# Latent and differential attention of a layer in one software pipeline of one stage, in place of two stages

## What is computed

```
def blocked_attention(q, k, v, scale):          # mla_group: 8 heads, 96 wide, values 64 wide
    def block(qb):
        s = jnp.einsum('bqhd,bkhd->bhqk', qb, k).astype(jnp.float32) * scale
        p = jax.nn.softmax(s, axis=-1).astype(v.dtype)
        return jnp.einsum('bhqk,bkhd->bqhd', p, v)
    return from_query_blocks(lax.map(block, to_query_blocks(q)))

def diff_group(dq, dk, dv, lam, lam_init, g_sub, cos, sin):   # 4 heads, 2 softmaxes each, 32 wide
    ...
    def block(qb):
        sc = jnp.einsum('bqhcd,bkhcd->bhcqk', qb, k).astype(jnp.float32) * scale
        p = jax.nn.softmax(sc, axis=-1)
        a = (p[:, :, 0] - lam * p[:, :, 1]).astype(v.dtype)
        return jnp.einsum('bhqk,bkhe->bqhe', a, v)
```

## Time and profile before

| | |
|---|---|
| median of 3 runs | 3117.5 us (3116.7 to 3121.64) |
| the profiled execution | 3118.45 us, of which its span in the profile is 3116.6 us |
| TensorE busy | 2902.9 us, 93% of the span |
| VectorE busy | 1549.0 us, 50% |
| ScalarE busy | 1204.4 us, 39% |
| GpSimd busy | 332.8 us, 11% |
| mean granted TensorE clock | 0.969 |

### The profile page before, as it was taken

The page is one execution under the profiler, slowest core; times in us unless marked ns, Lnnn a source line. Parts: engine busy times, 40 slices in busy tenths (PEclk is TensorE's granted clock), DMA queues, the critical chain, the costliest instruction groups (busy, mean ns, idle before and its releaser), DMA issues. The chain is left out here.

```text
span 3116.6 us, 38710 instructions
## 1 busy us (share of the span) xinstructions
PE 2902.9 (93%) x14576; PEld 2288.1 (73%) x14576; DVE 1549.0 (50%) x2177; ACT 1204.4 (39%) x1797; POOL 332.8 (11%) x286
## 2 busy tenths in 40 slices
PE   6999887999989999899899989999899899899998
PEld 2888765688868888586587768887675577678886
DVE  3467256565544443456753455443465663444434
ACT  3642434632233332434543343333424552333333
POOL 0010004500001100003000121100104001011100
PEclk8999999999999999999899999999999899999999
DMA  6100210045412222120032122222120131122232
GB/s 238 68 28 1 88 54 1 11 166 166 158 68 96 104 97 95 64 81 15 28 111 93 54 70 105 95 104 82 69 82 1 41 135 55 54 95 94 94 105 94
DMA packets 43552, 254.04 MB, mean 82 GB/s; under 512 B 4608, under 2 KB 6784, under 8 KB 15872
## 3 DMA queue, kind: packets, MB, share of 16 engines
q1 hardware_dynamic: 43392, 251.87, 22.7%
HBM read 249.75 MB, written 2.10 MB: 81 GB/s over the span
## 5 line engine op out<-in xcount | busy, mean ns | idle before, releaser
L250 DVE TENSOR_TENSOR ring_lo<-ring,ring_hi 128x2048 fp32r<-128x2048 f32 x201 | 460.7, 2292 | 796.3 <-ACT ring_hi L243 796.0
L243 ACT ACTIVATE ring_hi<-ring 128x2048 fp32r<-128x2048 f32 x201 | 383.8, 1909 | 462.1 <-PE bank L301 341.8
L301 PE MATMUL bank<-h_hi,ring_hi 128*128 128x512 f32 x1360 | 541.1, 398 | 19.4 <-DVE ring_lo L250 8.5
L301 PE MATMUL bank<-h_hi,ring_lo 128*128 128x512 f32 x1360 | 532.5, 392 | 0.0
L1435 PE MATMUL bank<-h_hi,ring_hi 128*128 128x512 f32 x960 | 374.1, 390 | 5.7 <-DVE ring_lo L250 5.7
L1439 PE MATMUL bank<-h_hi,ring_lo 128*128 128x512 f32 x960 | 373.5, 389 | 0.0
L1438 PE MATMUL bank<-h_lo,ring_hi 128*128 128x512 f32 x960 | 373.5, 389 | 0.0
L301 PEld LDWEIGHTS bank<-h_hi,ring_hi 128*128 128x128 f32 x1360 | 257.2, 189 | 79.4 <-issue 16.7
L301 PEld LDWEIGHTS bank<-h_hi,ring_lo 128*128 128x128 f32 x1360 | 257.1, 189 | 54.4
L301 PE MATMUL bank<-h_lo,ring_hi 128*128 128x512 f32 x624 | 243.9, 391 | 0.0
L1435 PEld LDWEIGHTS bank<-h_hi,ring_hi 128*128 128x128 f32 x960 | 180.2, 188 | 45.3 <-issue 5.5
(11 more groups left out here) (442 smaller groups left out, 4929.8 us busy)
## 6 DMA issues: line engine op xcount, KB each, us to landing
ring<-in_stream SPq DMA_DIRECT2D x209, 1024.0 KB, 4.8
mod_w<-in_stream SPq DMA_DIRECT2D x64, 256.0 KB, 4.6
xT<-in_xT SPq DMA_DIRECT2D x2, 2048.0 KB, 14.6
const<-in_const SPq DMA_DIRECT2D x1, 2306.5 KB, 15.7
par<-in_par SPq DMA_DIRECT2D x3, 696.0 KB, 4.0
memT<-in_memT SPq DMA_DIRECT2D x2, 1024.0 KB, 4.9
out<-xT SPq DMA_DIRECT2D x1, 2048.0 KB, 6.2
ctxT<-in_ctxT SPq DMA_DIRECT2D x1, 1024.0 KB, 4.9
```

The costliest lines, as they stand in the source:

```text
L243: nc.scalar.activation(self.slab_hi(slab + j), self.slab(slab + j), ACT.Copy).then_inc(slab_rounded, 1)
L250: nc.vector.tensor_tensor(lower, self.slab(slab + j), self.slab_hi(slab + j).bitcast(F32), ALU.subtract)\
L301: ins = nc.tensor.matmul(out, lhsT, rhs, start=start and w is w_hi and x is x_hi, stop=stop and w is w_lo)
```

## The change

`differential_attention` goes, and `two_attentions` takes its place, called once a layer instead of the two stages. In iteration i of one loop it issues a step of latent unit i or its predecessors and a step of differential unit i or its predecessors, on each engine. What each unit computes, and on which engine, stays. New buffers: the latent units have `probs` in the first half of `raw` and the differential ones in the second half (`raw` is free at this point; `squares2` isn't used any more), and a statistics tile each. PSUM is divided: banks 0 and 1 hold the scores of one latent unit, 2 and 3 those of one differential unit, bank 4 takes in turn the transposed tiles of latent head 0 and of the differential unit, bank 5 those of latent head 1, 6 and 7 the sums. So each kind has room for the scores of one unit instead of two. The score matmuls and maxima of the latent units signal head by head.

The diff, cut to its core (bodies of steps that only got new names are left out, and so are the removed lines, which stand in the listing above):

```diff
-        def differential_attention(name, dq, dk, dv, read_out, work, neg_lam):
+        def two_attentions(name, latent, dq, dk, dv, read_latent, read_diff, work, neg_lam):
             N = 4 * TB
-            S_ = lambda u: bank[:, 2 * (u % 2):2 * (u % 2) + 2, :]
+            probs, probsT, stat, diff_probs, diff_probsT, diff_stat = work
+            OUT, DIFF_OUT = 6, 7
...
             def tensor(pe):
                 def scores(u):
+                    for g in range(2):
+                        if u > 0:
+                            pe.wait_ge(exp_done.sem, exp_done.at(2 * (u - 1) + g + 1))
+                        lhsT, rhs = latent[u]["scores"][g]
+                        nc.tensor.matmul(bank[:, g, :], lhsT, rhs, start=True, stop=True).then_inc(scored.sem, 1)
+
+                def diff_scores(u):
                     n, tb, g = place_of(u)
-                    if u >= 2:
-                        pe.wait_ge(exp_done.sem, exp_done.at(u - 1))
+                    if u > 0:
+                        pe.wait_ge(diff_exp_done.sem, diff_exp_done.at(u))
...
                 def transposes(u):
+                    for g in range(2):
+                        pe.wait_ge(probs_ready.sem, probs_ready.at(2 * u + g + 1))
+                        if u > 0:
+                            if g == 0:
+                                pe.wait_ge(diff_out.sem, diff_out.at(u))
+                            else:
+                                pe.wait_ge(probs_out[1].sem, probs_out[1].at(u))
...
+                def diff_transposes(u):
+                    pe.wait_ge(probs_out[0].sem, probs_out[0].at(u + 1))
+                    pe.wait_ge(diff_ready.sem, diff_ready.at(u + 1))
...
+                def values(u):
+                    t, tb = divmod(u, TB)
+                    for g in range(2):
+                        pe.wait_ge(probs_out[g].sem, probs_out[g].at(u + 1))
...
+                for i in range(N + 2):
+                    if i < N:
+                        scores(i)
+                    if i >= 2:
+                        diff_transposes(i - 2)
+                        values(i - 2)
+                    if i < N:
+                        diff_scores(i)
+                    if 1 <= i <= N:
+                        transposes(i - 1)
+                    if i >= 3 and i % 2:
+                        diff_values(i - 3)
...
             def scalar(act):
...
+                for i in range(N + 1):
+                    if i < N:
+                        exps(i)
+                    if i >= 1:
+                        copy(i - 1)
+                    if i < N:
+                        diff_exps(i)
+                    if i >= 1:
+                        diff_copy(i - 1)
...
             def vector(dve):
...
+                for i in range(N + 2):
+                    if i >= 2:
+                        copy(i - 2)
+                        if (i - 2) % TB == 0 and i > 2:
+                            turn_out((i - 2) // TB - 1)
+                    if i < N:
+                        maxima(i)
+                    if 1 <= i <= N:
+                        differences(i - 1)
+                    if i < N:
+                        diff_maxima(i)
+                        inverses(i)
+                    if i == 2 * TB + 2:
+                        diff_turn_out(0)
+                turn_out(3)
+                diff_turn_out(1)
+
+            def gpsimd(pool):
                 for u in range(N):
+                    pool.wait_ge(inverse_ready.sem, inverse_ready.at(u + 1))
...
-                    paired_attention("latent", 4, unit_of, lambda t: mix[:, t, :],
-                                     (probs, spare[:, 0:4, :].rearrange("p (u h) n -> p u (h n)", u=2), stat), 2, (4, 5), (6, 7),
-                                     ("act", "dve"))
-                    differential_attention("differential", dq, dk, dv, lambda n: mix[:, 6 + n, :],
-                                           (probs, spare[:, 4:8, :], stat), neg_lam)
+                    two = lambda x, first: x[:, first:first + 4, :].rearrange("p (u h) n -> p u h n", u=2)
...
+                    two_attentions("attention", units, dq, dk, dv, lambda t: mix[:, t, :], lambda n: mix[:, 6 + n, :],
+                                   (two(raw, 0), two(h_spare, 0), stat, two(raw, 4), h_spare[:, 4:8, :], diff_stat), neg_lam)
```

More of the change, by code:

```diff
@@ L1279, in transposes @@
-                    if u >= 2:
-                        pe.wait_ge(probs_out.sem, probs_out.at(u - 1))
+                    for g in range(2):
[5 more added lines that the diff above has]
+                                pe.wait_ge(probs_out[1].sem, probs_out[1].at(u))
+                        for j in range(TB):
+                            last = nc.tensor.transpose(bank[:, 4 + g, j * P:(j + 1) * P], probs[:, u % 2, g, j * P:(j + 1) * P], con("ident"))
+                        last.then_inc(turned[g].sem, 1)
@@ L1286, in values @@
                 def values(u):
+                    t, tb = divmod(u, TB)
+                    for g in range(2):
+                        pe.wait_ge(probs_out[g].sem, probs_out[g].at(u + 1))
+                    if tb == 0 and t > 0:
+                        pe.wait_ge(sum_read.sem, sum_read.at(t))
+                    for j, sides in enumerate(latent[u]["values"]):
+                        for g in range(2):
+                            last = nc.tensor.matmul(bank[g * HD:(g + 1) * HD, OUT, tb * P:(tb + 1) * P], sides[g],
+                                                    probsT[:, u % 2, g, j * P:(j + 1) * P], start=j == 0, stop=j == TB - 1)
@@ L1293, in values @@
                                                     start=j == 0, stop=j == TB - 1)
                     if tb == TB - 1:
[L1295 to L1305, removed]
+                        last.then_inc(diff_summed.sem, 1)
@@ L1320, in scalar, with diff_copy @@
[L1320 to L1325, removed]
+                    act.wait_ge(turned[0].sem, turned[0].at(u + 1))
+                    nc.scalar.activation(probsT[:, u % 2, 0, :], bank[:, 4, :], ACT.Copy).then_inc(probs_out[0].sem, 1)
+                def diff_copy(u):
+                    act.wait_ge(diff_turned.sem, diff_turned.at(u + 1))
+                    nc.scalar.activation(diff_probsT[:, u % 4, :], bank[:, 4, :], ACT.Copy).then_inc(diff_out.sem, 1)
@@ L1343, in vector @@
                 nc.vector.memset(stat[:, :, :, :], 0.0)
+                nc.vector.memset(diff_stat[:, :, :, :], 0.0)
                 dve.drain()
[L1345 to L1353 removed]
```

120 lines of the change are left out of this document (77 added, 43 removed).

## The result

The changed kernel takes **3074.1 us** (median of 4 runs, 3072.5 to 3077.4), the kernel before 3118.8 beside it (3116.7 to 3121.6): a ratio of 0.9859, 95% interval 0.9848 to 0.9871. Measured again beside other kernels it took 3074.1, ratio 0.9859 (0.9844 to 0.9874).

A forecast was written before the change was run, and what follows sets the result against it. TensorE was taken to bound the first stage, VectorE the second, and TensorE the merged one: 16 x 6.01 + 2.3 = 98.5 us, saving 17.5 and 17.8, 35.3 together, giving 3082 us. The range was 3075 to 3097.

The forecast's parts named there:

- the waits (a) to (e): New stage: five TensorE waits, for differential and latent scores, latent transposes and two shared-bank copies, each taken as 0.
- An iteration is 3.81 + 2.20 = 6.01 us: New stage, TensorE: 3.81 us for a latent unit plus 2.20 for a differential unit make one iteration.
- The ways in and out, 2.3 us: New stage's edges: 0.9 us idle at the start, about 0.5 of waits and 0.9 through read-out at the end.
- VectorE has 1.16 us of room: New stage: VectorE needs 4.85 us an iteration against TensorE's 6.01, leaving 1.16.
- GpSimd and VectorE don't cost each other anything: New stage: VectorE's difference beside GpSimd's multiplying was taken to cost 0; upper end 2 x 1.03 us an iteration.
- the rival's price, 6.91 against 6.01: Every iteration: VectorE becomes the bound through GpSimd, 14.4 us a layer, 3111 us in all; chance 0.05.
- The clock stays up in the stage: New stage: TensorE at full clock, cost 0; upper end 6.8 us a layer.
- Behind the stage nothing is gained: Head of the next stage: no gain despite half clock, since TensorE waits there for VectorE's tiles.
- a next stage of another length as a sign of being wrong: Behind the new stage: a next stage taking another time than now would show the prediction wrong.
- the clock did not fall at the start: Rival, stage start: clock falls for 13.65 us a layer, costing 6.8 us each, 3096 us; chance 0.12.
- the pipelines do interleave: Rival said they don't: a ring of waits holds every iteration at about 7.1 us, 3118 us; chance 0.04.
- the 37% at half clock: Rival, new stage: clock as low as in the differential stage, 121 us a layer, 3128 us; chance 0.04.

The follow-up runs named there:

- e5: The changed kernel with one unused 128x512 matmul more on TensorE in 14 iterations of each layer: 3097.2 us, ratio 0.9928.
- e3: The changed kernel with the differential values moved directly behind the latent values on TensorE: 3069.1 us, ratio 0.9844; again 3070.3, 0.9846.
- e7: The changed kernel with three unused 128x512 reductions more on VectorE behind each unit's inverses: 3099.3 us, ratio 0.9935.
- e4: The changed kernel with VectorE's difference moved behind the unit's maxima and the inverse that releases GpSimd: 3151.1 us, ratio 1.0100.
- e10: The changed kernel with VectorE's difference moved behind the differential maxima but ahead of the inverses: 3083.8 us, ratio 0.9890.
- e1: The kernel before with unused TensorE matmuls in the differential stage, three at its start, one in each iteration, one at its end: 3107.6 us, ratio 0.9968.
- e2: The kernel before with only three unused TensorE matmuls, where the differential stage waits for its first exponentials: 3114.7 us, ratio 0.9986.
- e9: The changed kernel with differential values directly behind latent values and five unused 128x512 matmuls behind the stage's last values: 3076.2 us, ratio 0.9866.

## Why the prediction was right in kind and short in size

- *TensorE is the bound, and the waits (a) to (e) are hidden.* Right: no wait in 14 iterations, and e5's added work is paid in full.
- *An iteration is 3.81 + 2.20 = 6.01 us.* **The mis-sized term**: 5.87, which over 2 x 16 is 4.5 of the missing 9.3 us. The parts came from rows in which each group had another neighbour than it has now. The groups' slots, from start to start, are 1.72 for latent scores behind latent transposes, 1.82 behind differential values (as in the earlier trace rows, where every scores group stands behind values); 0.53 for differential transposes where the earlier trace rows gave 0.59, whose duration there stands behind a wait; 0.93 for latent transposes where the earlier trace rows gave 0.96, 1.02 ahead of differential values; 1.02 for values. e3 shows the same thing on purpose: two groups of values in a row take 0.93 + 0.97 us, 1.02 + 1.03 when each stands ahead of another kind. Why a group is dearer ahead of another kind, no run here tells.
- *The ways in and out, 2.3 us.* Right: 96.25 - 16 x 5.87 = 2.3, with 0.89 idle at the start (0.9 forecast), 0.33 of waits at the end (0.5) and 0.74 through the read-out (0.9). The stage is 96.25 where 98.5 was forecast.
- *VectorE has 1.16 us of room.* Right, 1.15 by e7, but with luck in the digits: it is 5.87 less 4.72 and not 6.01 less 4.85. Both terms were some 0.14 too high, VectorE's because it was a sum of durations, and those overlap: the maximum's row of 1.22 us has the inverse 1.14 behind its start.
- *GpSimd and VectorE don't cost each other anything.* The 0 was right, the reasoning and the picture were not. I expected the difference's operations longer by up to 1 us in a third of the iterations. No 128x512 operation was, and the one-column product by 0.3 us at most, in 3 of 16, since the inverse that starts GpSimd stands behind the difference in VectorE's order. And the rival's price, 6.91 against 6.01, added the lengthening to VectorE's sum; e4 beside e10 shows that it acts through a ring, at a price, with the clock that falls there, of 67 us and not 29.
- *The clock stays up in the stage.* Right, 1.00 in both layers. The falls of the earlier trace rows go with the waits beside them: e1, which fills these, has none, e4, which brings waits into the merged stage, has falls again. e2 shows that the first wait alone doesn't decide it.
- *"Behind the stage nothing is gained."* **The step that failed**, 2.6 + 0.9 us. I took TensorE to wait at 1550.58 for VectorE's tiles of 1549.59. The row at 1550.58 names no wait; in the trace after, the same product starts at 1528.01, ahead of VectorE's next tile (1529.66). So the products up to there don't wait for that tile, and their time is the clock's: the head is 12 products and one group, at half clock before until 1549.51, and it takes 4.2 us at the full one. e1 and e9, whose heads are at the full clock in both layers, show that by themselves. The prediction had named a next stage of another length as a sign of being wrong, and it was.
- Two small things: in layer 2 the forecast counted from a stage start 0.5 us ahead of the first row (2344.22 and 2344.72), which takes 0.5 back, and 1.8 us lie elsewhere, of which no step spoke.

With 5.87 and the heads the sum would have been 35.3 + 4.5 - 0.5 + 3.6 = 42.9 saved, and with the 1.8 it is the 44.6 measured. The iteration's own range (5.8 to 6.25) covered the first of these; what put the time below 3075 is the head, for which the range had no term (nor had it one for the 1.8).

Of the rivals, none came: the clock did not fall at the start, VectorE did not bind, the pipelines do interleave, and the 37% at half clock did not come over into a stage without waits.

## What to carry to other kernels

Two pipelines with different limits are worth interleaving; merging the stages alone brings nothing. The Trainium skill (Perfetto Trace Analysis, Optimization Strategy) says that where the most contended engine changes over time, interleaving those stretches may help; here it is some 30 of 44 us, if e1's 11, or a little more, are what the clock alone could give. Price a group of matmuls by the neighbours it will have, and a gain behind the stage by the clock it leaves, for the first microseconds of what follows too. When a cost lands on an engine with room, follow the ring it stands in (difference, transposes, scores, maximum, difference) before calling it hidden.

## What the hardware showed that I had not expected

Some of VectorE's operations beside GpSimd are not slowed but held. In e4 the one-column product at 1455.12 ends at 1456.12, as GpSimd's first 1.04 us end (1455.07 to about 1456.1), and the 128x512 scaling at 1456.05 takes 1.34 us instead of 0.48, until just past the end of GpSimd's second at 1457.11. In the trace after, VectorE's copies and latent maxima, which read the accumulation banks, run beside the same GpSimd operations at their usual 0.67 to 0.69 us. In e7 the added reductions, which read one on-chip tile, aren't held either: the three at 1454.18 take 1.85 us together, though GpSimd works from 1454.34 to 1456.38. The Trainium skill (SBUF — State Buffer, SBUF: two separate sides) calls the shared port pair an exclusive lock that whoever starts first holds for the whole instruction; the rows of e4 agree, even for an operation on 128x1. The Trainium skill (SBUF — State Buffer, Who interferes with whom) counts the scaling's kind of operation, which has one such tensor input, among those that can run in a two-port mode and so contend.
